# Expert weights in runs of two rows: 4 KB per lane, every second column in the transposes, and down pieces that split the contraction

## The chip, the cores and the metric

The kernel runs on one core of a Trainium2 chip. The metric is the device time of one execution in microseconds, lower is better. TensorE multiplies, VectorE, ScalarE and GpSimd work beside it, and SyncE issues most of the transfers.

## The reference

One decoder block on 1024 tokens of width 1024, in float32. A first half mixes a recurrent branch and an attention branch; this change does not touch it. The second half is a mixture of experts: 32 experts in 4 groups, each token goes to two experts of one group. What matters is this:

```
def expert_block(args):
    tok, e = args
    xb = x_pad[tok]
    hb = jax.nn.silu(xb @ w1[e]) * (xb @ w3[e])
    return hb @ w2[e]
...
'w_exp_gate': nrm(ks[19], (DEPTH, N_EXPERTS, D_MODEL, D_EXPERT), D_MODEL),
'w_exp_up': nrm(ks[20], (DEPTH, N_EXPERTS, D_MODEL, D_EXPERT), D_MODEL),
'w_exp_down': nrm(ks[21], (DEPTH, N_EXPERTS, D_EXPERT, D_MODEL), D_EXPERT),
```

`D_MODEL` is 1024 and `D_EXPERT` is 512, so each expert has three matrices of 2 MB. The results of a token's two experts are weighted and added, and a last norm follows.

## The kernel before

Stages run one after the other with a barrier between them. The last three are `route` (which token goes to which expert), `experts` and `combine`. Each engine has a written-out program that runs beside the others, and semaphores order them.

**Blocks and pieces.** An expert takes one block of 96 token slots; with this input 32 blocks are run, one per expert. Its weights come in six pieces of 1 MB: two each of gate, up and down. A piece is 128 lanes x 4 chunks x 512 columns. Of gate and up, whose rows are 512 long, a piece holds 512 of the 1024 contraction rows, and lane p of chunk k gets row 128 k + p, a run of 2 KB. Of down, whose rows are 1024 long, a piece holds one half of the columns of all 512 contraction rows, again in runs of 2 KB.

**The ring.** SyncE loads the pieces (`load_piece`, L1455) into a ring of 12 buffers (`e_raw`). Twelve pieces are loaded while `route` still runs. After that each load waits until TensorE has used the piece that lay in its buffer, twelve pieces earlier.

**The split.** Float32 products are made of three fast ones. ScalarE writes the rounded high part `e_h` (`piece_hi`, L1464; three buffers), VectorE writes the rest `e_l` in place of the raw piece (`piece_lo`, L1470), and TensorE multiplies rows-high by high, rows-high by low and rows-low by high (`piece_products`, L1486): 12 matmuls of 512 columns per piece, 72 per expert.

**One expert on TensorE** (`body`): up in two pieces, the first gate piece of the next expert, the transposes of the hidden rows (`turn_h`, L1554), the second gate piece, the first down piece, the transposes of the rows of the expert after the next (`turn_x`, L1534: eight of 96 x 128, from `e_xg`, which GpSimd gathers by index), and the second down piece. The result lies in two banks of `ps_y`, one per half of the columns.

**ScalarE after the last down piece** (`rows_out`, L1597 and L1599): it copies `ps_y` to `e_y`, issues its store to `y_d`, and only then takes the next `e_h`, that of the next expert's piece 4. That one needs a buffer which the last down piece held. The first two experts and the last two are written out; the 28 between them are 14 turns of a loop over pairs.

Two other loops serve as a comparison. `product` (L193) makes two matmuls in a row with the same stationary operand, which go to the two banks of a tile; `values` in the attention stage (L1007) changes the stationary operand with each matmul and stays in one bank, as `piece_products` does.

Of the kernel before, what the change touches and what calls it, by code (L numbers as in the profile page):

```python
# [33 lines left out]
P = 128  # L34
# [4 lines left out]
HALF = 512  # L39
# [15 lines left out]
MOST = -(-T // BLK)  # L55
MAXX = 2 * T // BLK + 2 * T // BLK % 2
RAW, SPLIT = 12, 3
SLOTS = (NE + MAXX) * BLK


# [29 lines left out]
class Kernel:  # L90
    def __init__(self, nc, ins, out):
# [10 lines left out]
        self.xn_d = dram("xn_d", (T, D))  # L102
        self.slots_d = dram("slots_d", (SLOTS + BLK, 1), I32)
        self.y_d = dram("y_d", (SLOTS, D))
        self.stage_sems = []
# [1341 lines left out]
    def load_piece(self, eng, piece, kind, half, e, first=False):  # L1447
        j, b, m = piece
        if not first:

            eng.wait_ge(self.e_used[m % SPLIT], 2 * j + m // SPLIT + 1 - RAW // SPLIT)
        w = self.ins["w_exp_" + kind][0][e].rearrange("(k p) n -> p k n", p=P)
        src = w[:, :, half * HALF:(half + 1) * HALF] if kind == "down" else w[:, 4 * half:4 * half + 4, :]
        slot, _ = self.raw_slot(piece)
        eng.dma_start(self.e_raw[slot][:, :, :], src).then_inc(self.e_in[slot], 16)  # L1455

    def piece_hi(self, act, piece):
        j, b, m = piece
# [18 lines left out]
    def piece_products(self, pe, ps, rows_h, rows_l, piece, first_piece, last_piece):  # L1477

        j, b, m = piece
        slot, _ = self.raw_slot(piece)  # L1480
        pe.wait_ge(self.e_lo[m % SPLIT], 2 * j + m // SPLIT + 1)
        w_h, w_l = self.e_h[m % SPLIT], self.e_l[slot]
        for k in range(4):
            for x, w, first, last in ((rows_h, w_h, k == 0, False), (rows_h, w_l, False, False),
                                      (rows_l, w_h, False, k == 3)):
                mm = pe.matmul(ps, x[:, k, :], w[:, k, :], start=first and first_piece, stop=last and last_piece)  # L1486
        mm.then_inc(self.e_used[m % SPLIT], 1)

    def experts(self):


        nc, k_ = self.nc, self
        work, high = Map(nc, self.raw_end, self.work_start), Map(nc, self.split_end, self.high)
        xg = [high.put(f"e_xg{b}", [BLK, D]) for b in range(2)]
# [5 lines left out]
        ht_h = high.put("e_hth", [P, 4, BLK], F32R)  # L1500
        ht_l = high.put("e_htl", [P, 4, BLK], F32R)
# [7 lines left out]
        ps_x, ps_h = by_chunk(k_.ps[0][:, :]), by_chunk(k_.ps[2][:, 0:HALF])  # L1509
        ps_g, ps_u, ps_y = k_.ps[1][0:BLK, 0:HALF], k_.ps[1][0:BLK, HALF:2 * HALF], k_.ps[3][0:BLK, :]  # L1510
        ident = k_.ident[0:BLK, 0:BLK]
# [18 lines left out]
        def turn_x(pe, j, b):  # L1530
            pe.wait_ge(gathered[b], 16 * (j // 2 + 1))
            pe.wait_ge(x_lo, j)
            for k in range(KD):
                mm = pe.transpose(ps_x[:, k, :], xg[b][:, k * P:(k + 1) * P], ident)  # L1534
            mm.then_inc(x_mm, 1)

        def gate(pe, j, b, half, piece):
# [19 lines left out]
        def down(pe, j, half, piece):  # L1557
            if half == 0:
                pe.wait_ge(h_lo, j + 1)
                pe.wait_ge(y_out, j)  # L1560
            k_.piece_products(pe, ps_y[:, half * HALF:(half + 1) * HALF], ht_h, ht_l, piece, True, True)

        def x_high(act, j, b, used):
            act.wait_ge(x_mm, j + 1)
# [54 lines left out]
        with nc.Block() as block:  # L1619
# [32 lines left out]
            @block.tensor  # L1652
            def _(pe):
                turn_x(pe, 0, 0)
                gate(pe, 0, 0, 0, (0, 0, 0))
                turn_x(pe, 1, 1)
                gate(pe, 0, 0, 1, (0, 0, 1))

                def body(j, b, last=False):
                    up(pe, j, b, 0, (j, b, 2))  # L1660
                    up(pe, j, b, 1, (j, b, 3))
                    gate(pe, j + 1, 1 - b, 0, (j, b, 4))
                    turn_h(pe, j)
                    gate(pe, j + 1, 1 - b, 1, (j, b, 5))
                    down(pe, j, 0, (j, b, 6))
                    if not last:
                        turn_x(pe, j + 2, b)
                    down(pe, j, 1, (j, b, 7))
# [6 lines left out]
                for h in range(2):  # L1675
                    down(pe, j, h, (j, b, 4 + h))
# [198 lines left out]
```

## Time and profile before

| what | value |
|---|---|
| median of 3 runs | 1959.67 us (1955.29 to 1959.69) |
| profiled execution, its own time | 1964.04 us |
| its span, first to last instruction | 1962.5 us |
| TensorE busy | 1738.7 us, 89% |
| VectorE busy | 1042.5 us, 53% |
| ScalarE busy | 846.8 us, 43% |
| mean granted TensorE clock | 0.957 |
| moved by DMA | 385.96 MB, 197 GB/s over the span |

The execution that was profiled took 1.5 us more than its span. A busy time counts an engine's instructions; matmuls overlap in the records, so their pace is to be read from the distance of their starts and not from the duration of one. The expert stage goes from about 1297 to 1910 us.

### The profile page before, as it was taken

The page shows a single profiled execution, that of the slowest core. Times are in us where ns is not written, and L with a number is a line of the kernel's source. Part 1 is how long each engine was busy: PE and PEld are TensorE (multiplying, and loading weights), DVE is VectorE, ACT ScalarE, POOL GpSimd, SP SyncE. Part 2 cuts the span into 40 slices and gives each one's busy share as a digit, 9 for nine tenths or more (in the row PEclk, how much of TensorE's full clock was granted, in tenths as well). Part 3 has the DMA queues.
Part 4 walks back from the last instruction along what each step waited for, and adds up shares of the span by engine and source line. Part 5 has one row for each costly group of instructions (what it writes and reads, how often), then busy time and mean ns, then how long its engine had stood idle before and what let it go on. Part 6 is the DMA issues. An engine that isn't in the chain of part 4 may idle for free. (4 is left out here: it accounts for less than half of the span.)

```text
span 1962.5 us, 23223 instructions
## 1 busy us (share of the span) xinstructions
PE 1738.7 (89%) x8639; PEld 1375.7 (70%) x8639; DVE 1042.5 (53%) x1123; ACT 846.8 (43%) x862; POOL 128.9 (7%) x170
## 2 busy tenths in 40 slices
PE   4999999999999999988869898569999999999980
PEld 3788888879977878767758798346666666666650
DVE  4343434342205013277764421468888888888866
ACT  5243434331212121155541202237777777777751
POOL 2100000000000000011110000010000000000005
PEclk9999999999999999999999999869999999999995
DMA  5722222222332232644433310859999999999927
GB/s 175 196 94 89 92 90 91 80 90 104 129 118 75 85 110 99 229 152 172 171 111 128 128 55 28 290 195 368 380 376 374 380 376 379 375 375 380 379 83 267
DMA packets 196202, 385.96 MB, mean 197 GB/s; under 512 B 11440, under 2 KB 70904, under 8 KB 192064
## 3 DMA queue, kind: packets, MB, share of 16 engines
q1 hardware_dynamic: 184064, 343.16, 48.9%
q0 software_dynamic: 8384, 29.63, 5.3%
q10 hardware_dynamic: 3712, 12.62, 1.7%
q8 instruction: 25, 0.41, 0.1%
q14 instruction: 17, 0.14, 0.0%
HBM read 317.95 MB, written 67.42 MB: 196 GB/s over the span
## 5 line engine op out<-in xcount | busy, mean ns | idle before, releaser
L1470 DVE TENSOR_TENSOR e_l<-e_raw,e_h 128x2048 fp32r<-128x2048 f32 x192 | 439.5, 2291 | 107.8 <-ACT e_h L1464 105.8
L1464 ACT ACTIVATE e_h<-e_raw 128x2048 fp32r<-128x2048 f32 x192 | 364.6, 1916 | 75.4 <-PE ps L1486 49.4
L193 PE MATMUL ps<-uh,w_h 128*128 128x512 f32 x1024 | 318.2, 392 | 21.5 <-DVE ul L834 13.6
L193 PE MATMUL ps<-ul,w_h 128*128 128x512 f32 x1024 | 317.1, 391 | 0.0
L193 PE MATMUL ps<-uh,w_l 128*128 128x512 f32 x1024 | 316.6, 391 | 0.0
L177 DVE TENSOR_TENSOR w_l<-w_raw,w_h 128x2048 fp32r<-128x2048 f32 x40 | 91.6, 2291 | 361.9 <-ACT w_h L173 361.9
L193 PEld LDWEIGHTS ps<-uh,w_h 128*128 128x128 f32 x1024 | 192.9, 189 | 63.6 <-issue 22.4
L1486 PE MATMUL ps<-e_h,e_xth 128*96 128x512 f32 x512 | 204.9, 400 | 27.3 <-DVE e_l L1470 25.4
L193 PEld LDWEIGHTS ps<-ul,w_h 128*128 128x128 f32 x1024 | 193.4, 189 | 40.6
L193 PEld LDWEIGHTS ps<-uh,w_l 128*128 128x128 f32 x1024 | 193.2, 189 | 40.5
L1486 PE MATMUL ps<-e_h,e_xtl 128*96 128x512 f32 x512 | 202.7, 396 | 0.0
L1486 PE MATMUL ps<-e_l,e_xth 128*96 128x512 f32 x512 | 202.3, 395 | 0.0
L173 ACT ACTIVATE w_h<-w_raw 128x2048 fp32r<-128x2048 f32 x40 | 76.5, 1913 | 285.5 <-DMA w_raw<-w_in 108.7
L205 PE MATMUL ps<-w_h,uh 128*128 128x256 f32 x512 | 148.6, 290 | 11.5 <-DVE ul L1143 5.8
L205 PE MATMUL ps<-w_l,uh 128*128 128x256 f32 x512 | 147.0, 287 | 0.0
L205 PE MATMUL ps<-w_h,ul 128*128 128x256 f32 x512 | 146.9, 287 | 0.0
L1486 PEld LDWEIGHTS ps<-e_h,e_xth 128*96 128x96 f32 x512 | 82.9, 162 | 72.9 <-issue 38.4
L205 PEld LDWEIGHTS ps<-w_h,uh 128*128 128x128 f32 x512 | 100.2, 196 | 14.6 <-issue 6.2
L1486 PEld LDWEIGHTS ps<-e_h,e_xtl 128*96 128x96 f32 x512 | 82.8, 162 | 35.6
L1486 PEld LDWEIGHTS ps<-e_l,e_xth 128*96 128x96 f32 x512 | 83.2, 163 | 32.0
L1486 PE MATMUL ps<-e_h,e_hth 128*96 128x512 f32 x256 | 103.3, 404 | 2.1 <-DVE e_htl L1592 2.1
L1486 PE MATMUL ps<-e_l,e_hth 128*96 128x512 f32 x256 | 101.9, 398 | 0.0
(246 smaller groups left out, 2167.7 us busy)
## 6 DMA issues: line engine op xcount, KB each, us to landing
e_raw<-w_exp_gate SPq DMA_DIRECT2D x64, 1024.0 KB, 8.6
e_raw<-w_exp_up SPq DMA_DIRECT2D x64, 1024.0 KB, 10.0
e_raw<-w_exp_down SPq DMA_DIRECT2D x64, 1024.0 KB, 10.1
w_raw<-w_in SPq DMA_DIRECT2D x28, 1024.0 KB, 5.5
qk_d<-qk SPq DMA_DIRECT2D x16, 1024.0 KB, 4.1
at_qk<-qk_d SPq DMA_DIRECT2D x8, 2048.0 KB, 8.8
y_d<-e_y ACTq DMA_DIRECT2D x32, 384.0 KB, 6.4
y_d<-zeros POOLq DMA_DIRECT2D x22, 384.0 KB, 11.0
```

What stands on the lines that cost most here:

```text
L173: act.activation(self.w_h[s][:, :, :], self.w_raw[s][:, :, :], ACT.Copy).then_inc(self.w_hi[s], 1)
L177: dve.tensor_tensor(self.w_l[s][:, :, :], self.w_raw[s][:, :, :], self.w_h[s][:, :, :].bitcast(F32), ALU.subtract).then_inc(self.w_lo[s], 1)
L193: mm = pe.matmul(ps[:, h * HALF:(h + 1) * HALF], w[:, k, :], u[:, k, h * HALF:(h + 1) * HALF], start=first, stop=last)
L205: mm = pe.matmul(ps, u[:, k, rows], w[s][:, k, :], start=first, stop=last)
L1464: act.activation(self.e_h[m % SPLIT][:, :, :], self.e_raw[slot][:, :, :], ACT.Copy).then_inc(self.e_hi[m % SPLIT], 1)
L1470: dve.tensor_tensor(self.e_l[slot][:, :, :], self.e_raw[slot][:, :, :], self.e_h[m % SPLIT][:, :, :].bitcast(F32), ALU.subtract).then_inc( ...
L1486: mm = pe.matmul(ps, x[:, k, :], w[:, k, :], start=first and first_piece, stop=last and last_piece)
```

## The change

Of gate and up, a lane now gets two consecutive rows of the matrix (`RUN = 2`), a run of 4 KB: chunk 2k+r of lane p holds row 256 k + 2 p + r. The rows of the tokens have to be in the same order, so `turn_x` reads every second column of `e_xg`. Of down, a piece now holds all 1024 columns of half of the contraction rows, one row of 4 KB per lane and chunk (`DOWN_RUN = 1`). Its products (`down_products`) go over two contraction chunks, three high/low pairs, and for each pair over the two halves of the columns, so that two matmuls in a row have the same stationary operand and alternate between the banks of `ps_y`; both down pieces add into both banks. Numbers of pieces, bytes, matmuls and transposes stay as they were.

```
+RUN, DOWN_RUN = 2, 1
...
-        w = self.ins["w_exp_" + kind][0][e].rearrange("(k p) n -> p k n", p=P)
-        src = w[:, :, half * HALF:(half + 1) * HALF] if kind == "down" else w[:, 4 * half:4 * half + 4, :]
+        run = DOWN_RUN if kind == "down" else RUN
+        lanes = self.ins["w_exp_" + kind][0][e].rearrange("(k p r) n -> p k (r n)", p=P, r=run)
+        n = lanes.shape[1] // 2
         slot, _ = self.raw_slot(piece)
-        eng.dma_start(self.e_raw[slot][:, :, :], src).then_inc(self.e_in[slot], 16)
+        eng.dma_start(self.e_raw[slot][:, :, :].rearrange("p (k r) n -> p k (r n)", k=n), lanes[:, n * half:n * half + n, :])\
+            .then_inc(self.e_in[slot], 16)
+
+    def lanes_of(self, row, chunk, run):
+
+        k, r = chunk // run, chunk % run
+        return row[:, k * P * run:(k + 1) * P * run].rearrange("t (p r) -> t r p", r=run)[:, r, :]
...
+    def down_products(self, pe, ps, ht_h, ht_l, piece, half):
+
+        j, b, m = piece
+        slot, _ = self.raw_slot(piece)
+        pe.wait_ge(self.e_lo[m % SPLIT], 2 * j + m // SPLIT + 1)
+        w_h, w_l = self.e_h[m % SPLIT], self.e_l[slot]
+        for k in range(2):
+            at = 2 * half + k
+            for x, w, first, last in ((ht_h, w_h, at == 0, False), (ht_h, w_l, False, False), (ht_l, w_h, False, at == 3)):
+                for c in range(2):
+                    mm = pe.matmul(ps[:, c * HALF:(c + 1) * HALF], x[:, at, :], w[:, 2 * k + c, :], start=first, stop=last)
+        mm.then_inc(self.e_used[m % SPLIT], 1)
...
-                mm = pe.transpose(ps_x[:, k, :], xg[b][:, k * P:(k + 1) * P], ident)
+                mm = pe.transpose(ps_x[:, k, :], k_.lanes_of(xg[b][:, :], k, RUN), ident)
...
-            k_.piece_products(pe, ps_y[:, half * HALF:(half + 1) * HALF], ht_h, ht_l, piece, True, True)
+            k_.down_products(pe, ps_y, ht_h, ht_l, piece, half)
```

## Rows read from the trace of the kernel before

**Rows 1.** Busy time, share of the span and instructions of each engine
```profile
PE 1738.7 (89%) x8639; PEld 1375.7 (70%) x8639; DVE 1042.5 (53%) x1123; ACT 846.8 (43%) x862; POOL 128.9 (7%) x170
```

**Rows 2.** Stretches of one expert each: length, busy by engine, clock, DMA share, GB/s
```profile
1325.56:1343.72 18.16, 17.77 (x85) 12.26 (x84) 15.45 (x10) 13.81 (x10) 1.41 (x1) 1.00 1.02 359
...
1600.81:1619.76 18.95, 17.92 (x88) 12.41 (x86) 15.60 (x10) 13.89 (x10) 1.40 (x1) 1.00 1.04 378
```

**Rows 3.** Waits from 1300 to 1880: total us, times, longest us
```profile
DVE e_l L1470 <- ACT e_h L1464: 102.4, 122, 5.3
...
PEld ps L1486 <- issue: 38.4, 30, 1.5
...
PE ps L1486 <- DVE e_l L1470: 25.4, 30, 1.1
```

**Rows 4.** Waits of SyncE's DMA queue, from 1300 to 1880
```profile
SPq L1455 <- PE ps L1486: 476.9, 180, 15.4
```

**Rows 5.** Timeline behind one last down piece: start us, us, engine, instruction, [idle before]
```profile
1610.12 1.02 ACT L1597 ACTIVATE e_y<-ps 96x1024 f32<-96x1024 f32 x1 [0.93 <-PE ps L1486]
...
1611.32 0.32 ACTq L1599 DMA_DIRECT2D y_d<-e_y  x1
...
1612.19 1.92 ACT L1464 ACTIVATE e_h<-e_raw 128x2048 fp32r<-128x2048 f32 x1 [1.04 <-issue]
...
1614.14 4.58 DVE L1470 TENSOR_TENSOR e_l<-e_raw,e_h 128x2048 fp32r<-128x2048 f32 x2 [2.45 <-ACT e_h L1464]
...
1615.15 0.40 PE L1486 MATMUL ps<-e_h,e_xtl 128*96 128x512 f32 x1
...
1616.58 0.45 PE L1486 MATMUL ps<-e_h,e_xth 128*96 128x512 f32 x1 [1.03 <-DVE e_l L1470]
```

**Rows 6.** Timeline of TensorE: transposes and second down piece of the same expert
```profile
1606.37 0.82 PE L1534 MATMUL ps<-ident,e_xg 96*128 96x96 f32 x8
1606.98 0.45 PE L1486 MATMUL ps<-e_h,e_hth 128*96 128x512 f32 x1
1607.27 0.40 PE L1486 MATMUL ps<-e_l,e_hth 128*96 128x512 f32 x1
...
1609.84 0.39 PE L1486 MATMUL ps<-e_h,e_xth 128*96 128x512 f32 x1
```

**Rows 7.** Timeline of TensorE in the product loop, pairs that share the stationary operand
```profile
300.02 0.62 PE L193 MATMUL ps<-uh,w_h 128*128 128x512 f32 x2
...
303.64 0.61 PE L193 MATMUL ps<-uh,w_l 128*128 128x512 f32 x2
```

**Rows 8.** Timeline of TensorE in the attention's value products, nine matmuls apart
```profile
966.58 0.40 PE L1007 MATMUL ps<-at_ptl,at_v 128*128 128x512 f32 x1
...
968.65 0.39 PE L1007 MATMUL ps<-at_ptl,at_v 128*128 128x512 f32 x1
```

**Rows 9.** Weight loads grouped by shape: busy us, mean ns of one, idle before
```profile
L1534 PEld LDWEIGHTS ps<-ident,e_xg 96*128 96x128 f32 x256 | 25.7, 145 | 18.6 <-DMA e_xg<-xn_d,slots_i 13.3 <-issue 0.2
...
L686 PEld LDWEIGHTS ps<-ul,f_h 128*8 128x8 f32 x16 | 1.4, 88 | 2.3
```

**Rows 10.** The 192 weight loads (line L1455), from issue to landing
```profile
DMA to landing us min/median/max: 5.5/9.9/14.6
```

**Rows 11.** Line L1599, the store of the rows, in ScalarE's queue: duration ns min/median/max
```profile
L1599 ACTq FUSED_REGOPS  x28: 51/51/57, 1366.8 to 1874.2; - x28
L1599 ACTq MOVE y_d<-e_y x28: 29/29/38, 1366.9 to 1874.3; - x28
```

**Rows 12.** ScalarE's high part behind the store: first expert, and one in the loop
```profile
1330.40 1.92 ACT L1464 ACTIVATE e_h<-e_raw 128x2048 fp32r<-128x2048 f32 x1 [0.49 <-ACT e_y L1597]
...
1630.82 1.92 ACT L1464 ACTIVATE e_h<-e_raw 128x2048 fp32r<-128x2048 f32 x1 [0.74 <-ACT e_y L1597]
```

**Rows 13.** DMA rate in 40 slices of the stretch from 1262 to 1300
```profile
GB/s 375 405 377 395 403 395 390 386 392 386 386 382 388 395 384 386 386 386 390 386 384 354 69 0 0 0 0 0 0 0 0 0 0 0 0 121 280 60 289 78
```

**Rows 14.** VectorE in the route stage, behind the first two weight loads
```profile
1239.55 2.48 DVE L1340 SCALAR_TENSOR_TENSOR rt_xn<-x,rt_rstd,rt_g 128x1024 f32<-128x1024 f32 x2 [6.72 <-DMA xn_d<-rt_xn]
```

## The prediction

> **What bounds the kernel now.** I read the page first: TensorE is busy 89% of the span, no other engine over 53% [rows 1]. An average over stages says little of one stage, so I cut the expert stage into stretches of one expert, from one gate load to the next. There the DMA share stands at its top (1.04, with 378 GB/s) beside TensorE at 17.92 of 18.95 us [rows 2]. Two resources look full, and the change speaks to both. Which of them sets the pace is told by the waits, and this is the reading on which everything else rests.
>
> The waits of the stage name no transfer: VectorE waits for ScalarE's `e_h`, TensorE for VectorE's `e_l` or its own queue [rows 3]. The loads wait for TensorE instead, all 180 of that stretch, 476.9 us in total [rows 4]. A load takes 5.5 to 14.6 us to land [rows 10]. It is issued when the piece twelve places before it has been used, and at six pieces per 18.95 us, 3.16 us each, it is wanted on TensorE 37.9 us later. Take three pieces off for the split on ScalarE and VectorE, 9.5 us, and 28.4 us of cover are left; the worst load uses 14.6. So the DMA is busy because it is fed early, and it is not what ends last.
>
> What ends last is a loop through three engines. After the last down matmul ScalarE copies the rows (start 1610.12, 1.02 us), issues the store (1611.32), starts the high part at 1612.19; VectorE starts the low part at 1614.14, and TensorE, which had the up pieces to do meanwhile and began its last one at 1615.15, goes on at 1616.58 [rows 5]. The last matmul of up would free it at 1615.38 (0.23 us after its start), so some 1.2 us are lost per expert. Everything from there to the next last down matmul is TensorE without a hole: gate, `turn_h`, gate, down, `turn_x`, down. **So the period is this stretch of TensorE plus a fixed chain, and a nanosecond in down or in `turn_x` counts in full**, 32 times. The up pieces lie under the chain and would not count.
>
> **The change part by part.**
>
> *The loads: 0.* They have 28.4 us of cover for at most 14.6. Twelve pieces are loaded during the routing, so the start of the stage does not see them either; it waits for the first gather. If this cover were gone they would cost what they run behind: a piece of 1.05 MB at 378 GB/s is 2.8 us against the 3.16 us that TensorE takes. In one place a load lies on the path: in the route stage VectorE waits 6.72 us for a store that was issued behind the first two gate pieces [rows 14]. Their 2.1 MB take about 5.4 us at the 386 GB/s of the full queue [rows 13]. The top of that strip is 405 GB/s, 5.2 us, so the gain is 0 to 0.3 us; the other end is a loss of the same size. I take 0. SyncE issues as many transfers as before, at the same places. GpSimd's gathers and ScalarE's stores share the engines with the loads and are hidden by two experts of lead.
>
> *The order inside down: minus 3.8 us.* Now 11 intervals from 1607.27 to 1609.84 give 2.57 / 11 = 233.6 ns per matmul [rows 6]. The nearest row for the new pattern is `product`: 16 matmuls in pairs from 300.02 to 303.64, 3.62 / 16 = 226.3 ns [rows 7]. It has 128 stationary columns where down has 96, so I looked for the old pattern with 128 columns: the value products take 2.07 / 9 = 230.0 ns [rows 8]. The pair is thus worth 3.7 ns by the one comparison and 7.3 ns by the other, of which a part may be the tile and not the pair. Down has 32 x 24 = 768 matmuls: 2.8 us to 5.6 us. I take 5 ns, 3.8 us. If what differs between the rows is something else, it is 0; a loss I exclude by `product`, which does exactly this at full clock.
>
> *The transposes with a step: 0.* The gathered rows are the stationary operand, so the step of two lies in the weight load. Eight transposes now cost 0.61 us, 76 ns each [rows 6]. No weight load in the trace reads with a step. The bound from below is nothing, since what is read stays 128 columns. From above I let each column take twice as long. A load of 8 columns takes 88 ns and one of 128 takes 145, so a column costs 57 / 120 = 0.475 ns [rows 9], and doubled over 128 columns that is 61 ns. All 256 transposes: 15.6 us, and they would lie on the path. A gain is excluded, as nothing is taken away. I take 0, for a reason that is weak: at 0.475 ns per column the load takes about one column per clock at 2.4 GHz, one 4-byte element from each lane, and I see no sign that neighbours are fetched together. This is the largest open term.
>
> The Trainium skill ("SBUF — State Buffer", "Door 1: The DMA port swizzle") says that the memory has lines of 16 bytes, and that a stride is free as long as two accesses fall into one line, up to four float32. A step of 8 bytes puts two into a line, so by that rule this term is 0; no run so far shows it.
>
> *What stays.* `turn_h`, the split on both engines, the copies out of PSUM and their semaphores are as they were. `ps_y` is complete only after the second down piece, but `rows_out` waited for that one before too, and the first down piece waits for the same copy of the expert before. Nothing new is waited for.
>
> **Sum.** 1964.04 us for the profiled execution, minus 3.8, gives 1960.2. That execution is 0.22% above the median of 1959.67, so on the median's scale the time is 1959.67 - 3.8 = 1955.9 us, a change of -0.19%. The runs before scatter over 4.4 us, so I take 0.3%, 5.9 us, as what a measurement of this kernel can tell from no change; the forecast lies inside.
>
> **The rivals.**
>
> *The step costs, slower.* One mechanism: the weight load of a stepped column takes two clocks in place of one. Its place is `turn_x`, between the down pieces, its price 15.6 us less the 3.8 of down: 1971.5 us. For it: nothing in the trace shows that a step is free. Against it: the 76 ns per transpose leave room over the 61 ns (128 x 0.475) of the load, so a part might hide. It decides the sign as soon as the step costs more than 15 ns per transpose (3.8 / 256), and reaches beyond 0.3% from 38 ns on. Chance 0.20.
>
> *The transfers set the pace after all, faster.* The first written-out expert took 18.16 us at 359 GB/s, one in the loop 18.95 at 378 [rows 2]. If the full DMA made the difference, fewer and longer runs could give it back: (18.95 - 18.16) x 28 = 22 us at most, and with odd turns at 18.7 rather about 18. That would be 1955.9 - 18 = 1938 us. Against it: the difference sits on ScalarE. Its gap behind the store is 0.49 us in the first expert and 0.74 in the loop, 1.04 at the turn of a pair [rows 5, 12], and just the 28 experts of the loop have register instructions there [rows 11]. Chance 0.07.
>
> The skill ("DMA: Bandwidth & Descriptors", "Why small descriptors are slow") gives about three cycles of overhead per packet beside one cycle per 32 bytes. By that 2 KB runs cost 67 cycles and 4 KB runs 131 in place of 134, an estimated 2% less DMA time. It would change the time only under this rival.
>
> *Down gains more than its pairs, faster.* If stationary reuse or the alternation saved 8 ns or more with 96 columns, 768 x 8 = 6.1 us, the change would pass 0.3%: about 1952 us. For it: 233.6 against 226.3 is already 7.3. Chance 0.12.
>
> *The longer runs slow the loads below demand, slower.* An expert needs 378 x 18.95 = 7.16 MB. At 360 GB/s it would take 19.9 us, 30 us over the stage: 1986 us. It decides from 378 GB/s downward, once the ring is drained; the full queue has only 386 [rows 13]. Against it: the bytes and lanes are the same, with fewer pieces. Chance 0.04.
>
> **How the numbers follow.** The forecast, a change between -0.3 and +0.3% with down a little faster and nothing else, has 0.57. It includes down at 0 (1959.7) and a step that costs up to 38 ns. Faster by over 0.3%: 0.07 + 0.12 = 0.19. Slower: 0.20 + 0.04 = 0.24. The range must take in the step at its bound (1971.5, with its scatter 1974) and down's far gain, and leaves out the two DMA cases with 0.11: 1948 to 1974 us. The likeliest case's own range is 1953 to 1962.
>
> **What the profile after would show.** Down's matmuls some 5 ns closer (about 228.5 ns from start to start), in pairs. `turn_x`'s eight transposes still 0.61 us, its weight loads near 145 ns; 200 ns would be the slower rival. The hole in front of the first gate matmul still about 1.2 us, with `e_h` behind the store as its cause. SyncE still waiting for TensorE, the landing shorter, the number of packets about half and the DMA share lower, with no time from it. The periods 0.12 us shorter. The prediction is wrong if the transposes stretch, or if the period falls by more than down's share of it; then look at the gap behind the store.

## The result and the profile after

The changed kernel is slower: median 1970.76 us against 1959.69 us, ratio 1.0048 with a 95% interval of 1.0025 to 1.007. That is 4.9 to 13.7 us lost. The forecast was 1955.9 us with no change that can be measured as the likeliest case; the time lies in the range of 1948 to 1974, the direction in the rival with 0.20, "the step costs", which gave 1971.5. The two medians lie 11.1 us apart and the two profiled executions 6.7 (1964.04 and 1970.76); the part of it that the expert stage accounts for is measured below.

The page of the kernel after, busy time by engine [rows 1], and a stretch of one expert in it [rows 2] (length, busy by engine, clock, DMA share, GB/s):

```profile
PE 1750.9 (89%) x8639; PEld 1390.1 (71%) x8639; DVE 1043.1 (53%) x1123; ACT 847.1 (43%) x862; POOL 123.5 (6%) x170
```
```profile
1604.17:1623.38 19.21, 18.19 (x88) 12.75 (x85) 15.60 (x10) 13.89 (x10) 1.15 (x1) 1.00 1.02 382
```

TensorE has 12.2 us more, with the same 8639 matmuls; VectorE and ScalarE have what they had. So the time is to be looked for on TensorE. The timeline of TensorE around the transposes of the same expert, which answers to [rows 6]:

```profile
1609.75 1.08 PE L1555 MATMUL ps<-ident,e_xg 96*128 96x96 f32 x8
1610.62 0.68 PE L1507 MATMUL ps<-e_h,e_hth 128*96 128x512 f32 x2
1611.14 0.63 PE L1507 MATMUL ps<-e_l,e_hth 128*96 128x512 f32 x2
...
1613.47 0.39 PE L1494 MATMUL ps<-e_h,e_xth 128*96 128x512 f32 x1
```

The eight transposes take 0.87 us to the next matmul, before it was 0.61. Down's pairs go at (1613.47 - 1611.14) / 10 = 233 ns per matmul, before 233.6. The transposes' own line in the kernel after (ns min/median/max) against [rows 9]:

```profile
L1555 PEld LDWEIGHTS ps<-ident,e_xg x256: 194/219/231, 1298.3 to 1877.1; 96*128 96x128 f32 x128
```

The waits of the stage in the kernel after, against [rows 3, 4]:

```profile
PE ps L1494 <- DVE e_l L1478: 24.5, 29, 1.1
```
```profile
SPq L1457 <- PE ps L1494: 333.9, 122, 14.6
SPq L1457 <- PE ps L1507: 150.9, 58, 3.3
```

The hole in front of the gate product is as large as it was, and loads still wait for TensorE, 484.8 us in all. They land in 8.2 us at the median, before in 9.9 [rows 10]. Packets fell from 196202 to 147050, and nothing waits less for it.

**How sizes are compared.** The time of one kernel varies by several us from run to run (the kernel before had 1951.78 to 1968.85 us in 35 runs), and in the profiles a good part of that arises before the expert stage: the first gate product starts at 1301.4 us in the kernel before and at 1295.1 us in e3, whose code up to there is the same but for the loads and the step of the first `turn_x`. So beside each ratio I give the distance from the third to the last group of `turn_x` transposes in the profile, 29 experts. In the kernel before it is 1869.40 - 1325.22 = 544.2 us, 18.76 per expert; after, 551.6 us, 19.02 per expert. The difference, 7.4 us, is 8.2 over 32 experts, and 32 x 0.26 is 8.3.

| kernel | ratio to before, 95% interval | 29 experts, us | loads | step |
|---|---|---|---|---|
| before | 1 | 544.2 | 2 KB | no |
| after | 1.0048 (1.0025 to 1.007) | 551.6 | 4 KB | yes |
| e1 step only | 1.0028 (1.0009 to 1.0047) | 551.4 | 2 KB | yes |
| e2 down only | 0.9986 (0.9968 to 1.0004) | 543.6 | down 4 KB | no |
| e3 runs only | 1.0030 (1.0011 to 1.0049) | 551.4 | gate, up 4 KB | yes |
| e4 rows permuted | 0.9981 (0.9964 to 0.9998) | 543.6 | 4 KB | no |
| e5 late copy | 0.9946 (0.9927 to 0.9965) | 534.1 | 2 KB | no |
| e6 late copy on e4 | 0.9934 (0.9909 to 0.9958) | 533.6 | 4 KB | no |
| e7 step of four | one run | 551.5 | 2 KB | four |
| e8 down 128 wide | one run | 545.0 | 4 KB | no |
| e9 later copy | 1.0078 (1.0059 to 1.0097) | 560.2 | 2 KB | no |
| e10 later copy on e4 | 1.0096 (1.0073 to 1.0118) | 559.8 | 4 KB | no |
| e11 later copy on after | 1.0121 (1.0096 to 1.0145) | 567.5 | 4 KB | yes |
| e12 early silu | 0.9898 (0.9877 to 0.9919) | 522.0 | 2 KB | no |
| e13 early silu on e4 | 0.9827 (0.9804 to 0.9849) | 512.5 | 4 KB | no |
| e14 early silu on after | 0.9899 (0.9875 to 0.9922) | 520.5 | 4 KB | yes |

### The profile page after: what moved, and what is told of

The parts are those of the page before. It is cut to its first block and busy times, and to the rows that moved or that the text cites. A ratio compares the mean times of both kernels' runs of the same rounds, so it can differ in the third digit from the quotient of the medians.

```text
span 1969.2 us, 23209 instructions
## 1 busy us (share of the span) xinstructions
PE 1750.9 (89%) x8639; PEld 1390.1 (71%) x8639; DVE 1043.1 (53%) x1123; ACT 847.1 (43%) x862; POOL 123.5 (6%) x170
## 2 busy tenths in 40 slices
DMA packets 147050, 385.96 MB, mean 196 GB/s; under 512 B 11440, under 2 KB 70904, under 8 KB 142912
## 5 line engine op out<-in xcount | busy, mean ns | idle before, releaser
L206 PEld LDWEIGHTS ps<-w_l,uh 128*128 128x128 f32 x512 | 100.2, 196 | 0.0
L206 PEld LDWEIGHTS ps<-w_h,ul 128*128 128x128 f32 x512 | 100.2, 196 | 0.0
```

The costliest lines, as they stand in the source:

```text
L206: mm = pe.matmul(ps, u[:, k, rows], w[s][:, k, :], start=first, stop=last)
```

## The experiments

### Which part of the change costs: e1 to e4

**e1**, the step alone, in the kernel before:

```
-                mm = pe.transpose(ps_x[:, k, :], xg[b][:, k * P:(k + 1) * P], ident)
+                mm = pe.transpose(ps_x[:, k, :], xg[b][:, (k // 2) * 2 * P:(k // 2 + 1) * 2 * P].rearrange("t (p r) -> t r p", r=2)[:, k % 2, :], ident)
```

> The kernel before with one edit: the transposes of the token rows read every second column, while the loads and the down products stay as before (the contraction then pairs tokens' columns and weight rows of different index, so the products are of other numbers; their count and form are the same). Theory A, the stepped weight load costs: the eight transposes take 0.87 us instead of 0.61 from the first of them to the next matmul, the weight load about 214 ns instead of 142, and the kernel is 8.3 us slower than before (32 x 0.26), ratio 1.0042. Rival B, the time comes from the loads or from down's order: the transposes are stretched but the kernel stays within 2 us of before, as the extra time is taken out of the hole in front of the gate matmul.

Here, in e7 and in e8 the operands no longer belong together, so their results are other numbers; what they take is comparable.

**e2**, down alone: `RUN, DOWN_RUN = 1, 1` in the changed kernel.

> The changed kernel with RUN = 1: gate and up are loaded and transposed as before, only down is loaded in whole rows of 4 KB and multiplied in pairs over the two banks. Theory A: no time is lost or gained by this part, ratio 1.000 with down matmuls at 232 ns from start to start, where the kernel before has 232 to 234. Rival B, down's order or its loads cost: slower than before by 3 us or more (ratio 1.0015 up). The prediction's own term, if the pair works after all: 2.8 to 5.6 us faster, ratio 0.997 to 0.9986.

**e3**, gate, up and the step alone: down is loaded and multiplied as before.

> The changed kernel with down loaded and multiplied as before, so that only the runs of two rows for gate and up and the stepped transposes are left. Theory A: 8.3 us slower than before, ratio 1.0042, the same as the step alone (e1) and as the whole change. Rival B, the longer runs of gate and up help or cost by themselves: it differs from the step alone by 2 us or more.

**e4**, everything but the step. The route stage writes the rows in the order of the lanes:

```
+                        for r in range(RUN):
+                            op = dve.scalar_tensor_tensor(
+                                out=xn[b][:, :].rearrange("t (k r p) -> t k r p", r=RUN, p=P)[:, :, r, :],
+                                in0=by_k(k_.x2[:, bass.ds(t, 1), :].rearrange("p a n -> p (a n)"))[:, :, :, r], ...
-                mm = pe.transpose(ps_x[:, k, :], k_.lanes_of(xg[b][:, :], k, RUN), ident)
+                mm = pe.transpose(ps_x[:, k, :], xg[b][:, k * P:(k + 1) * P], ident)
```

> The changed kernel, but VectorE writes the normed rows of the route stage with their columns already in the order of the lanes (two instructions of 512 elements, one per column parity, instead of one of 1024; the router's weight rows are loaded in the same order with two more small transfers), so the transposes in the expert stage read contiguous columns and the loads keep their runs of 4 KB. Theory A: the transposes are back at 0.61 us per eight and the 8.3 us are gone; what is left is the route stage's cost, eight times some 0.1 us for the second instruction plus what a step costs VectorE, at most 8 x 0.6 = 5 us if a step of two halves its rate; ratio 1.000 to 1.002. Rival B, the loads or down cost: still 6 us or more slower than before. Rival C, the transfers set the pace: faster than before by 3 us or more, since this version has all of the longer runs and no stepped transposes.

All three kernels with the step have 551.4 to 551.6 us for 29 experts, the three without it 543.6 to 544.2. That decides between the theories. The ratios of e1 and e3 (1.0028 and 1.0030) lie below theory A's 1.0042 with an interval that holds it, and also reach down to the 2 us of rival B in e1. The transposes' line in e1 and in e4:

```profile
L1534 PEld LDWEIGHTS ps<-ident,e_xg x256: 195/218/226, 1295.0 to 1873.2; 96*128 96x128 f32 x128
```
```profile
L1560 PEld LDWEIGHTS ps<-ident,e_xg x256: 137/140/230, 1295.1 to 1865.2; 96*128 96x128 f32 x128
```

With the loads of before, the step costs the same; with all of the long runs and no step, its cost is gone. Theory A holds in all four, rival B (loads or down cost) falls, and rival C of e4 (transfers set the pace) too: e4 has the same 543.6 us as e2, whose gate and up pieces come in 2 KB runs. In the route stage of e4 VectorE pays 2 x 746 ns per tile for 1281 ns, 1.7 us over eight tiles, and it still waits 7.7 us for stores beside it.

### What it is in the step that costs, and what the pairs are worth: e7 and e8

**e7**: as e1, with a step of four columns.

> As e1, but the transposes read every fourth column (16 bytes apart); the contraction pairs tokens' columns and weight rows of different index, with count and form unchanged. If what costs is that a weight load fetches more than one neighbouring float32 at a time and a step wastes the rest, the step of four costs more than that of two: weight loads near 330 to 380 ns, eight transposes near 1.4 us. If any step costs one fixed amount per column, the weight loads stay near 219 ns and the eight transposes at 0.87 us.

```profile
L1534 PEld LDWEIGHTS ps<-ident,e_xg x256: 195/217/230, 1293.8 to 1873.4; 96*128 96x128 f32 x128
```

217 ns, as with a step of two, and 551.5 us. Between these two steps the cost does not grow with the bytes that are skipped: it is 78 ns per load (218 - 140), or 0.6 ns per column if it arises column by column. All of these loads have 128 columns, so no run tells a cost per column from one per load, and none has a step beyond four. Not all of the 78 ns are seen: transposes come every 109 ns instead of every 76, so 33 of them lie on the path.

The Trainium skill ("SBUF — State Buffer", "Door 1: The DMA port swizzle") wants two accesses per 16-byte line for full rate, and puts the free stride at four float32. By the two accesses e1 would cost nothing and e7, with one per line, would cost; by the figure of four neither would. The runs disagree with both: the step of two costs 78 ns per load, and the step of four no more.

**e8**: the kernel of e4 with down's stationary operand 128 columns wide; its result goes to another pair of PSUM banks, which takes the 128 rows.

> The kernel of e4, but down's stationary operand is read 128 columns wide instead of 96 (the slice runs on into neighbouring columns, so result rows from 96 on are not used and for the last chunk the rows are shifted: other numbers, same count of matmuls). The pairs of the product loop take 226.5 ns per matmul with 128 columns, down's pairs 231.5 with 96. If the width of the stationary operand makes the difference, down falls to 226.5 ns. If it is what the other engines do beside it in the expert stage, it stays at 231 to 232.

Timeline of TensorE in e8:

```profile
1600.11 0.63 PE L1513 MATMUL ps<-e_l,e_hth 128*128 128x512 f32 x2
...
1601.96 0.62 PE L1513 MATMUL ps<-e_h,e_htl 128*128 128x512 f32 x2
```

1.85 us / 8 = 231 ns, so the width does not explain the 226.3 ns of `product` [rows 7]; over 29 experts e8 is even 1.4 us slower than e4. Nor does it seem to be what the others do meanwhile. The last four intervals of down in the kernel before, when no load runs (12 GB/s) and ScalarE and VectorE wait for this very result:

```profile
1906.61 0.39 PE L1486 MATMUL ps<-e_l,e_hth 128*96 128x512 f32 x1
...
1907.54 0.40 PE L1486 MATMUL ps<-e_h,e_htl 128*96 128x512 f32 x1
```

0.93 / 4 = 232.5 ns. What makes `product` 5 ns quicker stays open.

One premise of the pairs falls by the code and the counts. `piece_products` takes rows-high twice in a row, with the weights' high and low part, and `values` does the same with its high part. So neither changes its stationary operand with every matmul, as I had written of both; they change it in two of three. And a pair saves no load of it: TensorE has 8639 weight loads for its 8639 matmuls in both kernels, one for each, in `product` too. So the pairs change the order and the bank, and not the number of loads.

### Whether the long runs are worth anything: e5, e6, e9 to e14

The rest goes after the other half of the change. The loads have cover at this pace; do they have it at a faster one? For that the chain behind the last down product has to go.

**e5**, on the kernel before: ScalarE makes the next high part first and copies the rows out behind it.

```
+                def body(j, b, first=False, last=False, pair=None):
                     k_.piece_hi(act, (j, b, 4))
+                    if not first:
+                        rows_out(act, j - 1, 1 - b, (j, b, 1), (j - 1) // 2 if pair is None else pair)
...
-                    rows_out(act, j, b, (j, b, 7))
```

> The kernel before, with its loads of 2 KB runs, but ScalarE makes the high part of the next expert's piece 4 first and copies and stores the rows of the expert behind it (its program for experts 2 and 3 is written out too). Theory A, the hole in front of the first gate product is the chain copy, store, high part, low part, and TensorE sets the rest: the high part starts some 0.5 us after the last down matmul, the low part is ready after 4.7 us, before TensorE has finished its 5.5 us of up, and the hole of about 1.05 us goes: period 17.7 us instead of 18.76, up to 33 us faster. Then an expert's 7.16 MB need 405 GB/s where the full queue gave 386 in the kernel before. Theory A1, the transfers set the pace then: the period stops near 7.16 MB / 386 GB/s = 18.5 us, ScalarE waits for transfers, and the kernel is only 5 to 12 us faster. Rival B, something else fills the hole (VectorE's order): the period stays above 18.6 us without any wait for a transfer.

**e6**, the same on e4:

> The same order on ScalarE as in e5, on the kernel of e4: all loads in runs of 4 KB, columns permuted in the route stage, down in pairs. If the transfers set the pace in e5 (A1), longer runs are now worth something: by some 2% less transfer time per byte the period falls from 18.5 to about 18.1 us, 12 us over the stage beside the 3 us that e4 has. If they don't (A), e6 is as much faster than e5 as e4 is than before, about 0.2%, and both have a period near 17.7 us.

Each gains 10 us over 29 experts, not the 31 of theory A (29 x 1.06). A wait of e5 that the kernel before has not at this size:

```profile
PE ps L1554 <- DVE e_hid L1582: 15.9, 31, 0.6
```

The hole came up again in front of the hidden rows' transposes, about half a microsecond in each expert, and no wait of ScalarE in the expert stage names a load. So rival B of e5 is nearer the truth than A1, though the period, 18.42 us, fell below its 18.6. What did change is the landing of the loads, in e5 with 2 KB and in e6 with 4 KB:

```profile
DMA to landing us min/median/max: 5.5/13.2/16.8
```
```profile
DMA to landing us min/median/max: 4.8/9.9/18.8
```

The 13.2 us are the middle of a climb. By stretches of 100 us from 1350 on, e5's median landing is 10.2, 11.9, 13.3 and 15.1 us, while e6's stays at 9.8 to 10.0. An expert moves 7.07 MB (377 GB/s x 18.76 us in the kernel before, where landing does not climb). At 18.42 us e5 asks for 384 GB/s and gets 378 to 380. So its loads fall behind without anybody waiting yet: part of its gain is drawn from the ring.

**e9 to e11** put two high parts before the copy, on the kernel before, on e4 and on the changed kernel:

```
-                    k_.piece_hi(act, (j, b, 4))
+                    for m in (4, 5):
+                        k_.piece_hi(act, (j, b, m))
                     if not first:
                         rows_out(...)
                     act_silu(act, j, (j, b, -1) if not first else (0, 0, 1))
...
```

> As e5 (loads of 2 KB runs, nothing stepped), and ScalarE makes the high parts of pieces 4 and 5 before it copies the rows out, so that VectorE has the low part of piece 5 sooner and the hidden rows are ready when TensorE wants them. Theory A: the hole of some 0.5 us that e5 has in front of the hidden rows' transposes goes too, unless the transfers come in: an expert then needs 7.16 MB in 17.9 us, 400 GB/s. In e5, at 18.41 us and 378 to 379 GB/s in the stretches, the loads took 13.2 us to land and nobody waited for them. Theory A1, 2 KB runs top out near 380 to 386 GB/s: the period stays at 18.4 us and ScalarE's high parts wait for transfers. Without a top: period 17.9 us, 15 us faster than e5.

> The order of e9 on the kernel of e4 (all loads in runs of 4 KB, columns permuted in the route stage, down in pairs). In e6 these loads landed in 9.9 us at 387 GB/s. Theory A1: longer runs have the higher top, so the period falls to between 17.9 and 18.2 us and the kernel is 6 to 15 us faster than e9. Rival: the top is the same for both run lengths, or there is none; then e10 is faster than e9 by the 1 to 3 us by which e4 is faster than before.

> The order of e9 on the changed kernel as it is: runs of 4 KB and stepped transposes. Theory A1: the step's 0.26 us per expert is then partly paid back by the longer runs; the period is some 18.1 to 18.2 us, which is faster than e9 if the 2 KB runs top out at 18.4. Rival, no top that differs: 8 us slower than e10 and 5 to 8 us slower than e9.

All three expectations missed; the kernels are 15 to 24 us slower than before. The next gate product waits until `silu` has read this expert's gate result, and that now came last on ScalarE. The waits of e9 have the hole 15 times in this form, and 15 times with 21.4 us under "issue":

```profile
PE ps L1486 <- ACT e_silu L1576: 20.8, 15, 1.4
```

They say nothing of the loads, but the step shows once more: e11 has 567.5 us, e10 559.8.

**e12 to e14** keep the order of e9 but move that `silu` to where ScalarE is free, before the last down product has ended:

```
                     if not last:
                         x_high(act, j + 2, b, (j, b, 3))
+                    act_silu(act, j + 1, (j, b, 5))
...
```

> e9 failed because the gate product of the next expert waits until ScalarE has read the gate result of this one (silu), which e9 put behind two high parts and the copy. Here ScalarE takes that silu before the last down product is done, where it has 0.85 us free, and then the high parts of pieces 4 and 5, the copy and the store. Loads as in the kernel before, 2 KB runs. Theory A: no hole of TensorE is left but the restarts, period 17.8 to 17.9 us, which asks for 400 GB/s. A1, 2 KB runs top out at 380 to 386 GB/s: the loads' landing grows beyond the 13.2 us of e5, ScalarE waits for e_raw, and the period ends at 18.3 to 18.5 us, 1948 to 1953 us. If there is no such top: 1933 us.

> The order of e12 on the kernel of e4: all loads in runs of 4 KB, columns permuted in the route stage, down in pairs. A1: longer runs top out higher (some 2 to 4%, 395 to 400 GB/s), period 17.9 to 18.1 us, 6 to 15 us faster than e12. Rival, no difference in the top: as fast as e12 within 3 us.

> The order of e12 on the changed kernel as it is, with the stepped transposes. The step's 0.26 us per expert stays on TensorE: period 18.1 to 18.2 us. A1: that is at or below what 2 KB runs allow, so the change as it is would be as fast as e12 or up to 8 us faster. Rival, no difference in the top: 7 to 8 us slower than e12 and e13.

Here the transfers come in. In e12, with 2 KB runs, ScalarE waits for them in the expert stage, which it does in no other kernel here; 17.5 us more are for pieces of down:

```profile
ACT e_h L1464 <- DMA e_raw<-w_exp_up: 27.0, 23, 1.7
```

And stretches of 100 us in e12, e13 and e14 (busy by engine, then clock, DMA share, GB/s):

```profile
1500.00:1600.00 100.00, 100.00 (x476) 70.59 (x475) 88.78 (x52) 78.92 (x57) 8.29 (x6) 1.00 1.04 380
...
1700.00:1800.00 100.00, 96.08 (x454) 67.08 (x453) 82.27 (x48) 75.04 (x55) 14.38 (x6) 1.00 1.04 379
```
```profile
1700.00:1800.00 100.00, 100.00 (x480) 70.73 (x479) 88.58 (x52) 79.21 (x58) 8.80 (x7) 1.00 1.03 398
```
```profile
1700.00:1800.00 100.00, 100.00 (x470) 71.45 (x469) 87.31 (x52) 77.45 (x56) 6.78 (x6) 1.00 1.03 396
```

With 2 KB runs the rate stays at 378 to 380 GB/s from 1400 to 1800 us. At first the ring of twelve pieces covers the difference, TensorE is busy without a hole and an expert takes 17.7 us. The first hole stands at 1679 us, and from there on an expert takes 18.7 us, as long as 7.07 MB at 379 GB/s and hardly quicker than in the kernel before.

With 4 KB runs TensorE is busy throughout and the load queue still waits for it. The four windows of e13 have 397, 393, 393 and 398 GB/s, 395 on average. That is not all that the pace asks: 7.07 MB in 17.67 us are 400 GB/s. And the landing of e13 climbs, here from 1350 to 1450 and from 1650 to 1750 us:

```profile
DMA to landing us min/median/max: 8.2/9.7/11.0
```
```profile
DMA to landing us min/median/max: 13.9/15.2/16.3
```

So these loads fall behind too, only more slowly, and the 32 experts end before anybody waits. In e14, which asks for 394 GB/s, the landing stays at 8.8 to 9.2 us. The full queue can also be compared where no pace limits it, from 1262 to 1270 us, when hardly anything but the first twelve pieces is moved. The kernel before and the kernel after:

```profile
1262.00:1270.00 8.00, 0.68 (x8) 0.57 (x8) 5.66 (x20) 0.88 (x2) 0.00 (x0) 0.77 1.03 391
```
```profile
1262.00:1270.00 8.00, 0.76 (x9) 0.57 (x8) 5.22 (x19) 1.25 (x2) 0.00 (x0) 0.66 1.03 414
```

e1, e5 and e12 have 388 to 392 there, and e4, e6, e13 and e14 410 to 413. A1 holds: the longer runs have the higher top, by about 5% alone and by about 4% beside the gathers and stores (395 against 379). e13 takes 9.6 us less than e12 over 29 experts, of which down and the route stage explain 0.6 (e4 against the kernel before), and the intervals of the two ratios don't meet. Nearly all of it arises behind 1664 us, in nine experts with 0.6 to 1.1 us each. What holds 2 KB runs back is not settled: SyncE's issue of one load took 2.4 to 2.7 us at the median in e12, and 0.37 in e13 and e14. That tells of a full queue, and not whether packets or bytes fill it.

e14, the changed kernel in this order, is as fast as e12 over these 32 experts, and 8.1 us behind e13, by its step. It gets there by another way: its 17.95 us per expert hold to the end, where e12 ends at 18.7. The best version is e13, 1925.5 us, 1.7% faster than before. At 395 GB/s an expert would take an estimated 17.9 us once its cover is used up.

## Why the prediction was wrong

**The step that failed is "The transposes with a step: 0".** It should have been 32 x 0.26 = 8.3 us. Both bounds stood there, 0 and 15.6 us, and I took the lower for a reason that I called weak: that a unit-stride load takes about one column per clock. The upper bound came from the nearest rows. As a price of the load it was too low, 61 ns where 78 were measured; as a bound on the time it held only because 33 of the 78 lie on the path. The argument beside it, that a part might hide under the 76 ns of a transpose, was right: 45 of the 78 ns are hidden. With such bounds and no row for a stepped read, the forecast should have leaned on the end that a row supported.

**"The order inside down: minus 3.8 us" was mis-sized.** Both down pieces take 5.645 us in the kernel before and 5.62 in e2 and e4, 1 ns per matmul or 0.8 us. The pace of `product`, from another stage, did not carry over, and e8 excludes the width, which I suspected. The comparison also rested on a wrong reading of the code: the old order shares its stationary operand in part, and the new one saves no weight load. The sum with both terms put right is 1964.04 + 8.3 - 0.8 = 1971.5 us for the profiled execution; it took 1970.76.

**That the rival's 1971.5 us meets the median of 1970.76 is luck.** It priced the step at 15.6 us and down at 3.8, a loss of 11.8; the runs show 8.3 and 0.8, a loss of 7.5. The two errors partly cancel, and the rest lies within what the medians scatter by. That the time fell into the stated range says as little: the likeliest case in it was no change, and the runs show a loss.

**What held.** TensorE's stretch plus a fixed chain sets the period: 0.26 us in `turn_x` came out as 0.25 to 0.26 us of period, and the loads were free, since e2 and e4 differ only in gate's and up's runs (and in the route stage) and agree to 0.1 us. The rival "the transfers set the pace" falls for the kernel before: its loads land as fast at the end as at the start, they wait for TensorE, and longer runs brought nothing (e4). But I had it by a wide margin, and it falls by a thin one. I had set 2.8 us of transfer per piece against 3.16 us of TensorE, and left out the gathers and stores, which run on the same 16 DMA engines. With them an expert's 7.07 MB take 18.7 us at the 379 GB/s to be had, against a period of 18.76. The price of the loads is 0 only as long as the chain is left in. (The prediction's 7.16 MB took the rate of one of the longer turns for all.)

**One reading of my own falls.** A shorter landing is no proof of longer runs at work: e1, with 2 KB runs, lands gate's pieces in 7.3 us and the kernel before in 8.6; what differs is that its experts come more slowly, every 19.01 us instead of every 18.76.

From the three cycles per packet of the Trainium skill ("DMA: Bandwidth & Descriptors", "Why small descriptors are slow") the prediction estimated 2% for 4 KB instead of 2 KB. The runs show about 4% in the expert stage and 5% before it, and so agree in the sign and not in the size.

## What to carry to other kernels

A layout that makes a transfer better moves its disorder to whoever reads the data: put it where an engine waits anyway (here VectorE in the route stage), and not into an operand of the engine that sets the pace. Before costing a transfer at nothing, compare the rate it is asked for with the rate of a full queue, with all that shares it; if they are within a few per cent, the saving is not lost but locked behind the next faster schedule. A ring of buffers hides a queue that is too slow until it is drained, so look whether the landing climbs along the stage (e5, e13) before calling a gain lasting. And read every wait on a buffer before reordering an engine's program, as e9 shows.

## What was not expected of the hardware

Reading a stationary float32 operand with a step takes 218 ns for 128 columns instead of 140, and a step of four costs the same as one of two. The pace of matmuls of 512 columns, at a granted clock of 1.00, depends on the place in the kernel, 226.3 to 234 ns, which the width of the stationary operand does not explain. Every matmul had its own weight load (8639 of both), also where the operand was that of the matmul before. Loads in runs of 2 KB stopped at 379 GB/s beside gathers and stores and at 391 alone; those in runs of 4 KB reached 395 and 414.
